# The experts of a routed layer on one core: half-depth chunks, gathers shared by four experts, a second pass for slots 65 to 96

## Chip, core and metric
The kernel runs on one core of a Trainium2 chip, as one launch. The metric is the device time in microseconds. All data are f32. TensorE multiplies, VectorE (DVE in the rows) and ScalarE (ACT) read its results from PSUM, and SyncE (SP) issues nearly all transfers.

## What is computed
Two transformer blocks stand in a row, for 256 tokens of width 1024. The change touches only the mixture of experts in the second:

```
logits = xt @ w_router + b_router             # 256 tokens, 32 experts
top_val, top_idx = lax.top_k(logits, 4)
gates = softmax(top_val)
# for each expert e and its tokens xb:
hdn = xb @ w_up[e] + b_up[e]                  # 1024 x 2048
gate_h = minimum(hdn[:, :1024], 7.0)
up_h = clip(hdn[:, 1024:], -7.0, 7.0)
act = (up_h + 1.0) * gate_h * sigmoid(1.702 * gate_h)
y = act @ w_down[e] + b_down[e]               # 1024 x 1024
out[tok] += y * gate
```

Behind it come a layer norm and a gated product with `w_ple_gate`. The weights of one expert are 12.6 MB, those of all 32 are 403 MB of the 602 MB that the kernel reads.

## The kernel before
The blocks ahead of the experts are left as they are. At their end the router writes MSK (which token goes to which expert), POS (its slot in the expert, by a matmul with a triangle), GTE (its gate) and HTM, the tokens with the token index on the partitions. FLAG holds, for each expert, whether it has at most 64 tokens, and whether any has over 128. In that last case all engines branch to the `dense` code, which runs every expert on all 256 tokens. Else, for each expert, each engine branches to the narrow or to the broad form of `expert`. The narrow code of all experts lies in a row; the broad forms lie behind it, reached by a jump and left by another.

Weights come in chunks of 2 MB, six an expert: four of `w_up` and two of `w_down`. An up chunk c holds, for the full depth of 1024, 256 features (as pairs of gate and up columns), a down chunk 512 outputs. They go to a ring of eight places (parts of BIG, RG and SM1; `R.turn`, L1120). SP issues chunk i when `s_used` has reached i - 7 (L2834), that is when the chunk eight places earlier has been used. TensorE raises `s_used` after each chunk's products.

The narrow form, by TensorE's lines: L1198 puts the biases of two chunks into PSUM (32 rows deep). L1203 multiplies the 64 gathered tokens (stationary, 64 columns) with the chunk: the two halves of its columns go to partitions 0 to 63 and 64 to 127, as pairs of 64-wide tiles. After four chunks, L1157 turns the activations (`activated`), L1132 (`gather`, `picked`) picks the next expert's tokens by a product with SEL, L1214 turns SELG, which has the gates in it, and L1139 (`gather_turn`, `upright`) turns the picked tokens after ScalarE has copied them to XT. L1227 are the down products. L1239 scatters: YV times the turned SELG (SCT) is added to the output sums in banks 0 to 3 (`accap`). L1163 (`biases`) adds the down biases of all experts at once, in expert 24 (`BIASES`).

VectorE makes SEL for the next expert (`select`, L2520), SELG (L2537, L2540), the activation from each chunk (L2560, L2561, L2564, L2566) and the copies of turned blocks (L2569, L2571). ScalarE does the sigmoid (L1846), the copies of the gathered tokens (L1382, L1831) and of the down products to YV (L1852).

The broad form has 128 token slots: the products are 128 wide, unpaired, with 512 columns, and take the same weights twice as long. PSUM banks 4 to 7 serve all of this in turn (`take` waits for a bank to be free, `read_out` for a bank to be read).

Of the kernel before, what the change touches and what calls it, by code (L numbers as in the profile page):

```python
# [12 lines left out]
NEXP = 32  # L13
# [104 lines left out]
def build(nc, A, out):  # L118
    (T1, W1), (T2, W2) = smalls()
    ctx = ExitStack()  # L120
    with ctx:
# [16 lines left out]
        BD = sb("BDN", 1024, 32)  # L138
# [239 lines left out]
        BIASES = 24  # L378
# [8 lines left out]
        GTT = STAT[0:32, 1024:1280]  # L387
# [7 lines left out]
        XG = [XS_[:, 2048 + 1024 * i:3072 + 1024 * i].rearrange("p (k s) -> p k s", k=8) for i in range(2)]  # L395
        AV = CAT_[:, 0:1024]
        AVT = CAT_[:, 1024:2048]
        YV = CAT_[:, 2048:3072]
        XT = CAT_[:, 2560:3072]
        SEL = CAT_[:, 3072:3328].rearrange("p (a s) -> p a s", a=2)  # L400
        SELG = CAT_[:, 3328:3584].rearrange("p (a s) -> p a s", a=2)
# [34 lines left out]
        def _(pe):  # L436
# [673 lines left out]
            for tt in range(2):  # L1110
                m = pe.transpose(banks[b][0:32, tt * 128:tt * 128 + 128], GTE[:, tt, :], ID2)
# [10 lines left out]
            def expert_chunk(ex, c):  # L1122
                i = 6 * ex + c
                s, nth = R.get(("expert", ex, c), R.turn[i % 8])
                pe.wait_ge(s_landed[s], 16 * nth)
                return ring(s).rearrange("p (k n) -> p k n", k=8)

            def picked(b, part):

                for tt in range(2):  # L1130
                    for half in range(2):
                        m = pe.matmul(banks[b][64 * half:64 * half + 64, :], SEL[:, tt, 64 * part:64 * part + 64],  # L1132
                                      HTM[:, tt, 512 * half:512 * half + 512], start=tt == 0, stop=tt == 1)
                return m

            def upright(b):

                for i in range(4):
                    m = pe.transpose(banks[b][:, 128 * i:128 * i + 128], XT[:, 128 * i:128 * i + 128], ID2)  # L1139
# [7 lines left out]
            def gather_turn(ex):  # L1147
                read_out(("xt", ex))
                b = take(("xg", ex))
                upright(b).then_inc(s_full[b], 1)  # L1150

            def activated(ex, half, wd):
                b = take(("at", ex, half))
                pe.wait_ge(s_av, 4 * ex + 2 * half + 2)
                for i in range(wd // 128):
                    c, hh = (2 * half + i // 2, i % 2) if wd == 512 else (2 * half + i, 0)
                    m = pe.transpose(banks[b][:, i * 128:i * 128 + 128], AV[:, c * 256 + hh * 128:c * 256 + hh * 128 + 128], ID2)  # L1157
                m.then_inc(s_full[b], 1)

            def biases():  # L1160

                for d in range(8):
                    pe.matmul(accap(d), BD[0:32, d * 128:d * 128 + 128], GTT, start=False, stop=False, skip_group_check=True)  # L1163

            def half_of(b, h, sides):

                return banks[b][64 * h:64 * h + 64, 0:256] if sides == 2 else banks[b][:, :]

            def expert(ex, broad):
                Xg = XG[ex % 2]  # L1170
                cap = 128 if broad else 64
                sides = 1 if broad else 2
                wd = 512 if broad else 256
# [6 lines left out]
                if ex == BIASES:  # L1180
                    biases()
                read_out(("xg", ex))
                if broad:
                    b = F.pool[F.turn % 4]
                    pe.wait_ge(s_free[b], F.n[b])
                    pe.wait_ge(s_selg, ex + 1)
                    picked(b, 1).then_inc(s_more, 1)
                    pe.wait_ge(s_mcopy, 2 * ex + 1)
                    upright(b).then_inc(s_more, 1)
                    pe.wait_ge(s_mcopy, 2 * ex + 2)  # L1190
                for c in range(4):
                    if c % 2 == 0:
                        for q in c, c + 1:
                            b = take(("up", ex, q), quiet=True)
                            rows = slice(32 * q, 32 * q + 32)
                            onehot = ID2[rows, 32 * q + ex:32 * q + ex + 1].broadcast_to([32, cap])
                            for h in range(sides):
                                pe.matmul(half_of(b, h, sides), onehot, BUPR[rows, h * wd:h * wd + wd], start=True, stop=False)  # L1198
                    w = expert_chunk(ex, c)
                    b, n, m = F.at["up", ex, c]  # L1200
                    for k in range(8):
                        for h in range(sides):
                            i = pe.matmul(half_of(b, h, sides), Xg[:, k, 0:cap], w[:, k, h * wd:h * wd + wd], start=False, stop=k == 7)  # L1203
                            if not broad and c == h == 0 and k < 2:
                                i.then_inc(s_more, 1)
                    i.then_inc(s_used, 1)
                activated(ex, 0, wd)
                if ex + 1 < NEXP:
                    gather(ex + 1)
                activated(ex, 1, wd)  # L1210
# [5 lines left out]
                if ex + 1 < NEXP:  # L1216
                    gather_turn(ex + 1)
                T_ = AVT[:, 0:8 * cap].rearrange("p (k s) -> p k s", k=8)
                for c in range(2):
                    w = expert_chunk(ex, 4 + c)  # L1220
                    b = take(("dn", ex, c), quiet=True)
                    if c == 0:
                        read_out(("at", ex, 0))
                        read_out(("at", ex, 1))
                    for k in range(8):
                        for h in range(sides):
                            m = pe.matmul(half_of(b, h, sides), T_[:, k, :], w[:, k, h * wd:h * wd + wd], start=k == 0, stop=k == 7)  # L1227
                    m.then_inc(s_used, 1)
                read_out(("sc", ex))
                for c in range(2):  # L1230
                    read_out(("dn", ex, c))
                    for j in range(4):
                        if broad:
                            d, rows = 4 * c + j, slice(0, 128)
                            lh = YV[:, d * 128:d * 128 + 128]
                        else:
                            d, rows = 4 * c + 2 * (j % 2) + j // 2, slice(64 * (j % 2), 64 * (j % 2) + 64)
                            lh = YV[rows, c * 256 + (j // 2) * 128:c * 256 + (j // 2) * 128 + 128]
# [1662 lines left out]
def layout(inp):  # L2901
# [7 lines left out]
    A = {}  # L2909
# [67 lines left out]
```

## Time and profile before

| | us |
|---|---|
| median of 3 runs (2348.63 to 2351.63) | 2349.51 |
| span of the profiled execution | 2345.1 |
| TensorE busy (matmul) | 2265.2, 97% |
| VectorE busy | 815.0, 35% |
| ScalarE busy | 499.8, 21% |
| GpSimd busy | 154.2, 7% |
| HBM, mean over the span | 256 GB/s |

The span is from the first to the last instruction of one profiled execution, whose own total is not given beside it; the median lies 4.4 us above the span. The experts take the time from about 1347 us to 2304 us. A busy share of TensorE counts matmuls in flight. In the last third of the span the transfers run at 426 or 427 GB/s, above the 108 to 200 of most of the first half.

### The profile page before, as it was taken

How to read it: one execution, taken by the hardware profiler on the slowest of the kernel's cores; microseconds unless marked ns; L12 is line 12 of the kernel's file. 1: busy time of each engine (PE TensorE's matmuls, PEld its weight loads, DVE VectorE, ACT ScalarE, POOL GpSimd, SP SyncE). 2: the span in 40 equal slices, each digit the busy share in tenths (PEclk: the TensorE clock that was granted, in tenths of full speed). 3: DMA queues.
4: the chain of work that ended last, by engine and by line, in shares of the span. 5: the costliest groups of instructions: out<-in, count | busy, mean ns of one | idle time of the engine just before them, and what ended most of it. 6: DMA issues, size and time to landing. Idle time of an engine off the chain costs nothing.

```text
span 2345.1 us, 34269 instructions
## 1 busy us (share of the span) xinstructions
PE 2265.2 (97%) x14376; PEld 1662.3 (71%) x14376; DVE 815.0 (35%) x2072; ACT 499.8 (21%) x1180; POOL 154.2 (7%) x162
## 2 busy tenths in 40 slices
PE   7999999999999999999999999999999999999998
PEld 4777888888887788887688845666665555565556
DVE  2245554578425420005664321222222222222224
ACT  3255411100024432002443211111111111111113
POOL 1000111144301000000000000000000000000000
PEclk9999999999999999999999999999999999999999
DMA  9733223234325444344332777999999999999993
GB/s 376 276 108 108 108 72 108 72 126 162 108 84 200 182 177 148 144 150 180 131 143 109 295 288 310 426 427 425 427 427 426 427 427 426 427 426 426 427 426 124
DMA packets 44196, 601.60 MB, mean 257 GB/s; under 512 B 4704, under 2 KB 7392, under 8 KB 7808
## 3 DMA queue, kind: packets, MB, share of 16 engines
q1 hardware_dynamic: 43696, 595.40, 62.8%
q10 hardware_dynamic: 336, 3.87, 0.4%
q8 instruction: 120, 1.97, 0.3%
q14 instruction: 44, 0.36, 0.0%
HBM read 598.20 MB, written 1.05 MB: 256 GB/s over the span
## 4 chain that ended last, share of the span: by engine, by line
PE 82%; DMA 13%; DVE 2%; ACT 2%; issue 1%; POOL 0%; SPq 0%; POOLq 0%; PEldq 0%; DVEq 0%; ACTq 0%
PE PS L1203 14%; PE PS L957 8%; PE PS L1227 8%; DMA RG<-in_w_up 7%; PE PS L702 7%; PE PS L737 6%; PE PS L686 5%; PE PS L789 5%; DMA BIG<-in_w_up 4%; PE PS L650 3%; PE PS L535 3%; PE PS L775 2%; PE PS L1239 2%; PE PS L1132 2%; PE PS L474 2%; PE PS L1331 1%
## 5 line engine op out<-in xcount | busy, mean ns | idle before, releaser
L2560 DVE TENSOR_SCALAR STAT<-PS 128x128 f32<-128x128 f32 (+1 forms) x128 | 37.9, 296 | 668.4 <-PE PS L1203 668.4
L1203 PE MATMUL PS<-BIG,XS 128*64 128x256 f32 (+1 forms) x2016 | 236.3, 384 | 6.1 <-DMA BIG<-in_w_up 6.1
L1203 PEld LDWEIGHTS PS<-BIG,XS 128*64 128x64 f32 (+1 forms) x2016 | 145.2, 138 | 95.1 <-issue 17.9
L1203 PE MATMUL PS<-RG,XS 128*64 128x256 f32 (+1 forms) x1520 | 178.0, 384 | 12.2 <-DMA RG<-in_w_up 10.2
L957 PE MATMUL PS<-XS,RG 128*128 128x256 f32 x768 | 172.1, 382 | 5.0 <-DVE XS L1997 4.1
L1382 ACT ACTIVATE BIG<-PS 128x256 f32<-128x256 f32 (+2 forms) x197 | 82.2, 432 | 441.9 <-PE PS L702 138.9
L1203 PEld LDWEIGHTS PS<-RG,XS 128*64 128x64 f32 (+1 forms) x1520 | 107.9, 137 | 80.4 <-DMA RG<-in_w_up 15.8
L957 PEld LDWEIGHTS PS<-XS,RG 128*128 128x128 f32 x768 | 145.5, 191 | 26.9 <-issue 6.9
L1846 ACT ACTIVATE STAT<-STAT 128x128 f32<-128x128 f32 (+1 forms) x128 | 40.1, 313 | 570.2 <-DVE STAT L2560 570.2
L1963 DVE TENSOR_SCALAR HOLD<-PS 128x256 f32<-128x256 f32 x27 | 11.4, 423 | 382.0 <-PE PS L510 277.9
L686 PE MATMUL PS<-HN,RG 128*128 128x256 f32 x576 | 125.1, 379 | 1.0 <-ACT HN L1431 1.0
L1227 PE MATMUL PS<-BIG,CAT 128*64 128x256 f32 (+1 forms) x992 | 120.9, 387 | 0.1
L686 PEld LDWEIGHTS PS<-HN,RG 128*128 128x128 f32 x576 | 109.3, 190 | 16.5 <-issue 1.7
L789 PE MATMUL PS<-BIG,RG 128*128 128x256 f32 x512 | 110.7, 379 | 0.0
L789 PEld LDWEIGHTS PS<-BIG,RG 128*128 128x128 f32 x512 | 97.3, 190 | 13.2
L2700 POOL TENSOR_TENSOR HN<-HN 128x256 f32<-128x256 f32 x84 | 63.2, 753 | 631.7 <-ACT HN L1410 207.7
L1227 PEld LDWEIGHTS PS<-BIG,CAT 128*64 128x64 f32 (+1 forms) x992 | 73.6, 139 | 42.5 <-issue 10.0
L1227 PE MATMUL PS<-RG,CAT 128*64 128x256 f32 x768 | 86.4, 381 | 0.4 <-DVE CAT L2569 0.4
L1382 ACT ACTIVATE CAT<-PS 128x512 f32<-128x512 f32 (+2 forms) x74 | 32.7, 442 | 216.3 <-PE PS L789 103.8
L702 PE MATMUL PS<-HN,RG 128*128 128x256 f32 x336 | 77.3, 379 | 0.0
L1227 PEld LDWEIGHTS PS<-RG,CAT 128*64 128x64 f32 x768 | 54.2, 137 | 28.1 <-issue 3.1
L535 PE MATMUL PS<-HN,RG 128*128 128x256 f32 x320 | 73.1, 382 | 0.0
(374 smaller groups left out, 3427.9 us busy)
## 6 DMA issues: line engine op xcount, KB each, us to landing
BIG<-in_w_up SPq DMA_DIRECT2D x64, 2048.0 KB, 30.5
RG<-in_w_up SPq DMA_DIRECT2D x48, 2048.0 KB, 31.3
BIG<-in_w_down SPq DMA_DIRECT2D x32, 2048.0 KB, 32.0
RG<-in_w_ff SPq DMA_DIRECT2D x31, 2048.0 KB, 8.1
RG<-in_w_ada SPq DMA_DIRECT2D x24, 2048.0 KB, 8.3
RG<-in_w_down SPq DMA_DIRECT2D x24, 2048.0 KB, 34.5
RG<-in_w_in SPq DMA_DIRECT2D x23, 2048.0 KB, 8.2
SM<-in_w_up SPq DMA_DIRECT2D x16, 2048.0 KB, 31.3
```

The source lines that it names most:

```text
L474: m = pe.matmul(banks[b][32 * g:32 * g + 32, :], SILK[:, 32 * k:32 * k + 32], w[:, k, :], start=k < 4, stop=k >= 4)
L535: m = pe.matmul(banks[b][:, 0:256], w[:, k, c0:c0 + 128], N[:, k, :], start=k == 0, stop=k == 7)
L650: m = pe.matmul(banks[b][:, 0:256], w[:, k, 128 * (n % 4):128 * (n % 4) + 128], own(CAT, s)[:, k, :], start=i == 0, stop=i == 7)
L686: m = pe.matmul(banks[b][:, 0:256], w[:, k, 128 * n:128 * n + 128], own(HN, s)[:, k, :], start=k == 0, stop=k == 7)
L702: m = pe.matmul(banks[b][:, 0:256], w[:, k, :], a[:, k, :], start=not first and k == 0, stop=k == 3, skip_group_check=True)
L737: return pe.matmul(banks[b[j]][:, 256 * half:256 * half + 256], w, a, start=first and half == 0, stop=last, skip_group_check=True)
L789: m = pe.matmul(banks[b][:, 0:256], w[:, k, :], own(FFH, s)[:, k, :], start=k == 0, stop=k == 31)
L957: m = pe.matmul(banks[b][:, 0:256], w[:, k, 128 * n:128 * n + 128], src[:, k, 0:256], start=k == 0, stop=k == 7)
L1203: i = pe.matmul(half_of(b, h, sides), Xg[:, k, 0:cap], w[:, k, h * wd:h * wd + wd], start=False, stop=k == 7)
L1227: m = pe.matmul(half_of(b, h, sides), T_[:, k, :], w[:, k, h * wd:h * wd + wd], start=k == 0, stop=k == 7)
L1382: i = act.activation(dst, banks[b][rows, part], fn)
L2700: S.up(pool.tensor_tensor(H[:, i, :], H[:, i, :], H[:, k, :], ALU.add))
```

## The change
In words:

- An up chunk now holds half of the depth (512) for 512 gated features (1024 columns), a down chunk half of the depth for all 1024 outputs. The products keep their pairs of 64-wide tiles, now with 512 columns instead of 256. Two chunks fill one PSUM bank together.
- The gather puts 256 features of the tokens of four experts into XG in one group of four 128-deep matmuls, already the right way up, and is done once an expert (`gather((ex,), ex % 4)`): of the four experts held in XG, one is replaced, a quarter at a time. There is no turning any more. Ahead of the loop three such gathers run, the fourth in the second chunk of expert 0.
- An expert with 65 to 96 tokens does its first 64 as all do, and the others in a second pass with four 32-wide tiles (`more_picked`, `more_upright`, `more_biases`, `more_up`, `more_turned`, `more_down`, `more_scatter`). Over 96 tokens lead to the dense code.
- The scatter of an expert runs in the next expert's head, behind its upper biases. YV is copied in one piece of 512 columns.
- The down biases are added ahead of the loop (`lower_biases`), from 128 partitions.

```diff
-            def gather(ex):
-                pe.wait_ge(s_sel, ex + 1)
-                b = take(("xt", ex))
-                picked(b, 0).then_inc(s_full[b], 1)
+            def gather(key, j):
+
+                b = take(("xg",) + key)
+                for i in range(2):
+                    for tt in range(2):
+                        m = pe.matmul(banks[b][:, 256 * i:256 * i + 256], HTM[:, tt, 256 * j + 128 * i:256 * j + 128 * i + 128],
+                                      SEL[:, tt, :], start=tt == 0, stop=tt == 1)
+                m.then_inc(s_full[b], 1)
+
+            def lower_biases():
+
+                for j in range(2):
+                    for q in range(4):
+                        rows = slice(32 * q, 32 * q + 32)
+                        pe.matmul(accap(2 * q + j), BD[rows, 128 * j:128 * j + 128], GTT[rows, :], start=j == 0, stop=False,
+                                  skip_group_check=True)
+
+            def upper_biases(ex):
+
+                for s in range(2):
+                    b = take(("up", ex, s), quiet=True)
+                    for h in range(2):
+                        q = 2 * s + h
+                        rows = slice(32 * q, 32 * q + 32)
+                        pe.matmul(banks[b][64 * h:64 * h + 64, :], ID2[rows, 32 * q + ex:32 * q + ex + 1].broadcast_to([32, 64]),
+                                  BUPR[rows, :], start=True, stop=False)
...
+            def more_up(b, c, w):
+
+                xg = XG2.rearrange("p (k s) -> p k s", k=8)
+                for kk in range(4):
+                    for q in range(4):
+                        part = w[:, kk, 512 * (q // 2):512 * (q // 2) + 512].rearrange("p (g n) -> p g n", g=2)
+                        m = pe.matmul(banks[b][32 * q:32 * q + 32, 256 * (c // 2):256 * (c // 2) + 256], xg[:, 4 * (c % 2) + kk, :],
+                                      part[:, :, 128 * (q % 2):128 * (q % 2) + 128], start=False, stop=c == 3 and kk == 3,
+                                      skip_group_check=True)
                 return m
...
+                upper_biases(ex)
...
                 if broad:
-                    b = F.pool[F.turn % 4]
...
+                    more_picked(ex, b2)
+                if ex:
+                    scatter(ex - 1)
+                    read_out(("xg", ex - 1))
...
+                if broad:
+                    more_upright(ex, b2)
+                    more_biases(ex, b3)
                 for c in range(4):
...
+                    for kk in range(4):
...
+                        for h in range(2):
+                            i = pe.matmul(banks[b][64 * h:64 * h + 64, :], XG[:, 4 * (c % 2) + kk, 64 * r:64 * r + 64],
+                                          w[:, kk, 512 * h:512 * h + 512], start=False, stop=c % 2 == 1 and kk == 3)
...
+                        i = more_up(b3, c, w)
                     i.then_inc(s_used, 1)
...
+                pe.wait_ge(s_av, 2 * ex + 1)
+                activated(take(("at", ex, 0)), 0)
+                if broad:
+                    pe.wait_ge(s_mcopy, 7 * ex + 3)
                 if ex + 1 < NEXP:
-                    gather(ex + 1)
-                activated(ex, 1, wd)
+                    pe.wait_ge(s_sel, 2 + min(ex, NEXP - 5))
+                    gather((ex,), ex % 4)
...
+                if broad:
+                    more_turned(ex, b2)
+                    pe.wait_ge(s_mcopy, 7 * ex + 6)
...
-                dve.tensor_copy(XT, banks[b][:, :]).then_inc(s_mcopy, 1)
...
+            for j in range(3):
+                gather(("first", j), j)
...
-            gather_turn(0)
+            lower_biases()
...
-            dve.tensor_scalar(FLAG[0:1, 32:33], SV[0:1, 410:411], 128.0, None, ALU.is_gt).then_inc(s_flag, 1)
+            dve.tensor_scalar(FLAG[0:1, 32:33], SV[0:1, 410:411], 96.0, None, ALU.is_gt).then_inc(s_flag, 1)
```

VectorE forms the activation twice an expert on 256 columns instead of four times on 128, and in an expert with over 64 tokens a third time for the second pass. Its `select` makes one operation of 2 x 64 columns with the slot number compared to POS, which holds zero for a token that isn't routed to the expert. The number of bytes is the same in all transfers.

## Rows read from the trace of the kernel before

**Rows 1.** Busy time by stretch of the experts: engines, clock, DMA share, GB/s.
```profile
core 0: us, PE busy (x) PEld busy (x) DVE busy (x) ACT busy (x) POOL busy (x), PEclk, DMA share, GB/s
1343.00:1443.00 100.00, 93.93 (x490) 49.48 (x490) 22.75 (x76) 13.00 (x27) 0.00 (x0) 0.99 0.67 256
1443.00:1812.00 369.00, 366.74 (x3200) 222.93 (x3196) 85.40 (x306) 42.29 (x106) 0.00 (x0) 1.00 1.01 426
1812.00:2288.00 476.00, 452.04 (x3888) 272.32 (x3888) 102.45 (x367) 51.28 (x128) 0.00 (x0) 1.00 1.01 427
```

**Rows 2.** The chain that ended last: start us, us, what (experts 4, 14 and 30).
```profile
1493.37 7.06 PE PS L1203 x64
...
1779.16 33.05 DMA RG<-in_w_up
...
2252.64 35.69 DMA RG<-in_w_up
```

**Rows 3.** Timeline, SP's issues: start us, us, line, what.
```profile
1424.09 7.19 SPq L2795 DMA_DIRECT2D BIG<-in_w_up  x2
1441.27 3.78 SPq L2795 DMA_DIRECT2D RG<-in_w_up  x2
...
1459.57 13.36 SPq L2795 DMA_DIRECT2D BIG<-in_w_up  x4
```

**Rows 4.** Timeline, TensorE in narrow expert 4 and the head of expert 5.
```profile
1508.37 1.94 PE L1132 MATMUL PS<-XS,CAT 128*64 128x512 f32 x8
...
1510.24 0.44 PE L1157 MATMUL PS<-MODT,CAT 128*128 128x128 f32 x2
...
1518.65 2.00 PE L1239 MATMUL PS<-STAT,CAT 64*128 64x256 f32 x16
...
1520.58 0.66 PE L1198 MATMUL PS<-CAT,MODT 32*64 32x256 f32 x8
...
1521.17 3.67 PE L1203 MATMUL PS<-RG,XS 128*64 128x256 f32 x32
```

**Rows 5.** Timeline, from the first selection to the first chunk.
```profile
1346.32 0.54 DVE L2520 TENSOR_SCALAR CAT<-HOLD,MISC 128x64 f32<-128x64 f32 x2
...
1347.11 1.94 PE L1132 MATMUL PS<-XS,CAT 128*64 128x512 f32 x8 [0.87 <-DVE CAT L2520]
...
1351.67 7.13 PE L1203 MATMUL PS<-BIG,XS 128*64 128x256 f32 x64
```

**Rows 6.** Timeline, TensorE where the broad expert 1 begins and ends.
```profile
1377.02 2.00 PE L1239 MATMUL PS<-STAT,CAT 64*128 64x256 f32 x16
1378.95 1.94 PE L1132 MATMUL PS<-XS,CAT 128*64 128x512 f32 x8
...
1430.76 3.62 PE L1239 MATMUL PS<-STAT,CAT 128*128 128x256 f32 x16
...
1434.30 0.66 PE L1198 MATMUL PS<-CAT,MODT 32*64 32x256 f32 x8
...
1438.43 6.26 PE L1203 MATMUL PS<-RG,XS 128*64 128x256 f32 x54 [2.03 <-issue]
```

**Rows 7.** 32-wide tiles (timeline), and full matmuls of 256 columns (chain).
```profile
21.69 1.92 PE L474 MATMUL PS<-RG,SM 128*32 128x512 f32 x16 [0.64 <-DMA RG<-in_w_ada]
...
1250.32 3.46 PE PS L957 x16
```

**Rows 8.** Timeline, VectorE's activation chain and a ScalarE eviction in expert 1.
```profile
1406.35 0.42 DVE L2560 TENSOR_SCALAR STAT<-PS 128x256 f32<-128x256 f32 x1 [6.38 <-PE PS L1203]
...
1407.67 0.42 DVE L2566 TENSOR_TENSOR CAT<-HOLD,STAT 128x256 f32<-128x256 f32 x1
...
1430.96 0.60 ACT L1852 ACTIVATE CAT<-PS 128x512 f32<-128x512 f32 x1 [6.27 <-PE PS L1227]
```

**Rows 9.** Timeline, the last chunk's products in expert 31.
```profile
2298.15 3.67 PE L1227 MATMUL PS<-SM,CAT 128*64 128x256 f32 x32
```

**Rows 10.** Instruction queue in 1812 to 2288 us: packets, MB, share.
```profile
q8 instruction: 32, 0.52, 0.4%
```

More of the change, by code:

```diff
@@ L1160, in biases @@
[L1160 to L1167, printed above, removed]
+                return ring(s).rearrange("p (k n) -> p k n", k=4)
+            def gather(key, j):
[5 more added lines that the diff above has]
+                m.then_inc(s_full[b], 1)
@@ new lines, in activated, with scatter @@
+            def activated(b, s):
+                for i in range(2):
+                    m = pe.transpose(banks[b][:, 128 * i:128 * i + 128], AV[:, 256 * s + 128 * i:256 * s + 128 * i + 128], ID2)
+                m.then_inc(s_full[b], 1)
+            def scatter(ex):
+                read_out(("sc", ex))
+                read_out(("dn", ex))
+                for j in range(4):
+                    for h in range(2):
+                        rows = slice(64 * h, 64 * h + 64)
+                        m = pe.matmul(accap(4 * h + j), YV[rows, 128 * j:128 * j + 128], SCT[rows, :], start=False,
+                                      stop=ex == NEXP - 1, skip_group_check=True)
+                m.then_inc(s_scat, 1)
@@ new lines, in more_turned, with more_down @@
+            def more_turned(ex, b):
+                pe.wait_ge(s_mcopy, 7 * ex + 5)
+                for s in range(2):
+                    pe.transpose(banks[b][:, 128 * s:128 * s + 128], AV2[:, 128 * s:128 * s + 128], ID2)
+                for tt in range(2):
+                    m = pe.transpose(banks[b][:, 256 + 128 * tt:384 + 128 * tt], SELG2[:, tt, :], ID2)
+                m.then_inc(s_more, 1)
+            def more_down(b, c, w):
+                for kk in range(4):
+                    for q in range(4):
+                        m = pe.matmul(banks[b][32 * q:32 * q + 32, 0:256], TS2[:, 128 * c + 32 * kk:128 * c + 32 * kk + 32],
+                                      w[:, kk, 256 * q:256 * q + 256], start=c + kk == 0, stop=c == 1 and kk == 3)
+                return m
@@ L1169, in expert, with more_scatter @@
+            def more_scatter(ex):
+                pe.wait_ge(s_mcopy, 7 * ex + 7)
+                for j in range(2):
+                    for q in range(4):
+                        rows = slice(32 * q, 32 * q + 32)
+                        pe.matmul(accap(2 * q + j), YV2[rows, 128 * j:128 * j + 128], TS2[rows, 256:512], start=False, stop=False,
+                                  skip_group_check=True)
             def expert(ex, broad):
-                Xg = XG[ex % 2]
-                cap = 128 if broad else 64
@@ L1172, in expert @@
[L1172 to L1173 removed]
+                r = ex % 4
                 if ex + 1 < NEXP:
@@ L1224, in expert @@
                         read_out(("at", ex, 1))
-                    for k in range(8):
-                        for h in range(sides):
-                            m = pe.matmul(half_of(b, h, sides), T_[:, k, :], w[:, k, h * wd:h * wd + wd], start=k == 0, stop=k == 7)
-                    m.then_inc(s_used, 1)
[L1229 to L1238, printed above, removed]
-                        m = pe.matmul(accap(d), lh, SCT[rows, :], start=ex == 0 and d % 2 == 0, stop=ex == NEXP - 1,
-                                      skip_group_check=True)
@@ L1241, in expert @@
-                m.then_inc(s_scat, 1)
+                    for kk in range(4):
+                        i = 256 * c + 128 * (kk % 2) + 64 * (kk // 2)
+                        for h in range(2):
+                            m = pe.matmul(banks[b][64 * h:64 * h + 64, :], AVT[:, i:i + 64], w[:, kk, 512 * h:512 * h + 512],
+                                          start=c + kk == 0, stop=c == 1 and kk == 3)
+                    if broad:
+                        read_out(("at", ex, 1))
+                        m = more_down(b4, c, w)
@@ L1863, in dense @@
                     act.activation(SG[:, f % 2, :], GH[:, f % 2, :], ACT.Sigmoid, scale=1.702).then_inc(s_dsg, 1)
-            gathered(0)
+            for j in range(3):
+                gathered(("first", j), j)
             act.wait_ge(s_flag, 1)
@@ L2570, in expert @@
+                for s in range(2):
+                    b = full(("at", ex, s))
+                    dve.tensor_copy(AVT[:, 256 * s:256 * s + 256], banks[b][:, 0:256]).then_inc(s_free[b], 1)
                 b = full(("sc", ex))
                 dve.tensor_copy(SCT, banks[b][:, 0:256]).then_inc(s_free[b], 1)
+                if broad:
+                    dve.wait_ge(s_more, 3 * ex + 3)
+                    dve.tensor_copy(TS2, banks[b2][:, :]).then_inc(s_mcopy, 1)
+                    dve.wait_ge(s_used, 6 * ex + 6)
+                    dve.tensor_copy(YV2, banks[F.at["at", ex, 1][0]][:, 0:256]).then_inc(s_mcopy, 1)
```

278 lines of the change are left out of this document (142 added, 136 removed).

## Prediction

> **What bounds the kernel now.** I read the stretches first. From 1443 us to 2288 us the DMA engines are busy all the time at 426 to 427 GB/s, while TensorE is busy 367 of 369 us before 1812 and only 452 of 476 us after [rows 1]: two limits lie close together, and the second half is the transfers' alone. The chain says the same: the up chunk on which TensorE waits until 1812.2 was issued at 1779.2, the one it waits for until 2288.3 was issued at 2252.6 [rows 2]. Between those two landings lie 16 experts, 96 chunks of 2 MB: 476.1 / 96 = 4.96 us a chunk, 29.76 us an expert. TensorE's own period is 27.8 us (expert 4's first product at 1493.37, expert 5's at 1521.17) [rows 2, 4]. So work saved inside a narrow expert only lengthens its wait for the next chunk.
>
> What can move the end is when the stream becomes gapless. Chunk i is issued when chunk i-8 has been used. Issue time less 4.96 i is largest where the last gap ends: chunk 18 issued at 1424.09 gives 1334.8, chunk 20 at 1441.27 gives 1342.1 [rows 3]; the chunks behind give less (24, issued at 1459.57, 1340.5). Hence the end of the stream hangs on the moment at which the first chunk of expert 2 is used. Between 1343 and 1443 the DMA share is only 0.67 [rows 1]: expert 1, the only one with over 64 slots, runs 128 wide and unpaired, 53.7 us from 1377.02 to 1430.76 [rows 6], against 29.8 us of transfers.
>
> **The change, part by part, as a shift of the issue of chunk 20.** Times are of the profiled execution (span 2345.1 us); the median 2349.51 us lies 4.4 us above the span, and I carry that over.
>
> Start. Selection becomes two 256-wide VectorE operations of 0.42 [rows 8] in place of two of 0.27 [rows 5]: +0.3. Before, 4.56 us pass from the first gather matmul at 1347.11 to the first chunk at 1351.67 [rows 5]. New: three gathers of four 256-column, full-depth matmuls. Sixteen records of that form, 8 matmuls, take 3.46, so 0.432 each [rows 7] and 1.75 a gather with its edge: 5.2. The lower biases (8 matmuls, 32 deep, 128 wide) follow, then the upper biases (4, 512 columns). Four 32-deep matmuls of 256 columns take 0.59 (1520.58 to 1521.17) [rows 4], so four overlap, with 0.16 at the edge: 1.0 for each of the two. Together 7.2, so +2.6. If the lower ones did not overlap, 3.5 instead of 1.0. First use: +2.9.
>
> Expert 0. Added: the fourth first gather 1.75, and the rolling gather 1.75 where the old gather took 1.87 (1508.37 to 1510.24). Gone: the second bias group 0.59 and the turning 0.6. The products stay at four half-width pairs' worth of columns: 7.0 for two chunks (7.06 in [rows 2]); half as many weight loads save at most 0.1 each two. Sum +0.4, so chunk 13's issue +3.3.
>
> Expert 1. From the last down product of expert 0: upper biases 1.0, 32-wide picking 1.0, scatter 1.95 [rows 4], turning 0.45, second biases 1.0: 5.4. Each chunk is 3.5 of 64-wide pairs plus 16 matmuls 32 wide in fours. Are fours concurrent? Eight 32-wide matmuls of 512 columns take 1.92; one after another they would take 8 x 0.86 = 6.9 [rows 7]. So 4 x 0.43 + 0.2 = 1.9, a chunk 5.45 and not 7.0; six are 32.7. Between up and down: turning 0.36, a new wait of TensorE on VectorE (the activation chain of the second half, 1.74 + 0.12 [rows 8], and two more reads of 0.42 of the 65-to-96 bank) some 2.4, gather 1.75, turnings 1.3, a wait of about 0.9 for the TS2 copy (estimate, from 0.60 for a 512-column ScalarE eviction [rows 8]). Behind the down products: YV2 copy 0.6 and the second scatter 1.0. Sum 5.4 + 32.7 + 6.7 + 1.6 = 46.4 against 53.7: -7.3. Queued behind the new waits are the down products and thus the issue of chunks 18 and 19; they give 1330 by the rule above and stay uncritical.
>
> Expert 2's head. Before: unpaired scatter 3.54, biases 0.59, 2.03 of "issue" after the return from the broad code, first chunk: 10.4 to the issue at 1441.2 [rows 3, 6]. New: 1.0 + 1.95 + 2.03 + 3.5 = 8.5: -1.9.
>
> Issue of chunk 20: 3.3 - 7.3 - 1.9 = -5.9. The bounds: all waits of the broad body covered, -9; two more stalls of the 2.03 kind and the slower biases, +1.
>
> Stream. The narrow expert has 134 matmul records where it had 242. The instruction queue moved 0.52 MB in the 16 experts of that stretch [rows 10], TensorE's part perhaps 0.4. Halving it frees 0.2 MB, 0.5 us at 427 GB/s, 0.9 over the stage: -0.9 (0 to -1.2).
>
> Tail. The last chunk's products end 3.67 after 2298.15 [rows 9]; the last up chunk to the first down product takes some 0.3 more (VectorE's chain is 256 wide), covered by the two landings of 4.96 between. Before, the scatter began at once, since half of YV was out. Now it waits for one 512-column eviction, 0.60 + 0.15: +0.8. Only in the last expert is it bare; in the others the next upper biases (1.0) hide it, and where they don't, it costs up to 0.75 of TensorE's slack. That slack grows: new TensorE period 14.0 + 0.36 + 1.75 + 0.77 + 7.0 + 1.0 + 1.95 = 26.8, so 2.9 us under the 29.76. The biases at expert 24 leave, worth nothing there. SP only follows uses; its order, POOL and the ending stay.
>
> Sum: -5.9 - 0.9 + 0.8 = -6.0, so 2339.1 us of span, 2343.5 us.
>
> On tiles: [rows 7] shows fours of one shape overlapping within one group. The Trainium skill, "TensorEngine Tiling (Array Packing)", Key Properties, says that changing the tiling mode drains the engine; the new chunk of expert 1 changes it twice, 12 times in all. The 0.16 to 0.22 us by which groups exceed their columns' time in the trace agree with a small drain, so by the rule too the sum stays.
>
> **The rivals.**
> (a) The gain is eaten at the front: same within 0.2%. The fork into the sparse code had an eviction to hide behind; now biases follow directly, and the broad body is longer. Each stall of the 2.03 kind [rows 6] is a third of the gain. Two, or the bare lower biases, give -6.0 + 2.5 to 4.1: 2346 to 2347.6. For it: such a stall exists. Against: the first operation of the broad code (1378.95) follows the scatter before it (1377.02 and 1.95) without a gap [rows 6]. Chance 0.30. The Trainium skill, "Runtime: NRT & Kernel Launch", Instruction fetch mechanics, says that a taken branch out of the fetched window costs a stall; the 2.03 agrees.
> (b) Slower: the 32-wide fours lose their overlap when mixed with 64-wide pairs in expert 1. There are 24 fours in its chunks. Serial, each costs 1.3 more, +31, so 2374. It decides from 0.44 us more a four (10.7 us in all, for +0.2%). Against: [rows 7]. Chance 0.08.
> (c) The change doesn't do what it says: over 96 slots in an expert the dense code runs. Dense costs 192 full matmuls of 0.432, 83 us, an expert, so some +1700. The routing worked out from the reference gives at most 76 slots (expert 1), and the trace shows one broad expert. Chance 0.01.
> (d) More: broad waits covered and no stall on return, -9 to -11: 2338.5 to 2340.5. Chance 0.08.
> The forecast, 2340.5 to 2345, has 0.53.
>
> **The numbers.** 0.2% is 4.7 us, about what a measurement can tell: the line is 2344.8. Nearly all of the forecast and (d) lie below it: faster 0.60; (a) and the forecast's rim: same 0.30; (b), (c) and an unforeseen +11: slower 0.10. Range 2338.5 to 2350.5: it takes (d) and (a) and leaves (b) and (c) out.
>
> **What would show it.** Chunk 20 issued near 1435.4 with the first chunk used near 1358.2; expert 1 from last down product to YV2's scatter 46 us, its chunks 5.45; TensorE's first wait for a chunk by expert 12 instead of 15; 4.95 us a chunk between landings; last scatter 0.8 later behind its products. It is wrong if a later chunk than 20 becomes the critical one, if the chunks of expert 1 exceed 5.9, or if the pace of the stream changes by more than 0.02 us a chunk (3.4 us over the 172 left).

## The result and the profile after

| us | before | changed |
|---|---|---|
| median (lowest to highest) of 4 runs each | 2349.07 (2346.01 to 2351.63) | 2331.05 (2329.14 to 2332.87) |
| span of the profiled execution | 2345.1 | 2329.2 |
| TensorE busy, matmuls | 2265.2, 97% | 2224.1, 95% |
| instructions | 34269 | 27569 |

The ratio is 0.9925, 95% interval 0.9911 to 0.9939: by it the changed kernel is 17.6 us faster (14 to 21; the two medians lie 18.0 apart), where 6.0 was forecast. The direction held, the size was too small by a factor of two to three, and the time lies below the range.

The span fell by 15.9 us. I cut it at four moments that both traces have: the first gather matmul; the issue of chunk 20; the moment at which TensorE gets the last up chunk (chunk 189); the end. The rows of the changed kernel (timeline; start us, us, then as before):

```profile
1344.83 5.42 PE L1138 MATMUL PS<-CAT,XS 128*128 128x256 f32 x24 [0.73 <-DVE CAT L2693]
1350.18 1.15 PE L1147 MATMUL PS<-STAT,BDN 32*128 32x256 f32 x16
1351.26 1.09 PE L1157 MATMUL PS<-CAT,MODT 32*64 32x512 f32 x8
1352.27 3.65 PE L1275 MATMUL PS<-BIG,XS 128*64 128x512 f32 x16
...
1430.60 3.76 SPq L2888 DMA_DIRECT2D RG<-in_w_up  x2
...
2271.60 3.65 PE L1275 MATMUL PS<-RG,XS 128*64 128x512 f32 x16 [1.24 <-DMA RG<-in_w_up]
```

and that of the kernel before for the third moment (the others are in [rows 5, 3]):

```profile
2288.38 1.95 PE L1203 MATMUL PS<-RG,XS 128*64 128x256 f32 x16 [1.23 <-DMA RG<-in_w_up]
```

| stretch | before | changed | difference | forecast |
|---|---|---|---|---|
| start to first gather | 1347.11 | 1344.83 | -2.3 | 0 |
| first gather to issue of chunk 20 | 94.16 | 85.77 | -8.4 | -6.2 |
| issue of chunk 20 to last up chunk | 847.1 | 841.0 | -6.1 | -0.9 |
| last up chunk to end | 56.7 | 57.6 | +0.9 | +0.8 |

(The -6.2 is the forecast's -5.9 less the +0.3 that lies ahead of the first gather.) The first line is code that the change leaves alone. The router's 32 matmuls took 6.74 us in one trace, at a granted clock of 0.70, and 5.12 in the other, at 0.95; that is 1.6 of the 2.3 us:

```profile
1335.26 6.74 PE L1089 MATMUL PS<-SM,HN 128*128 128x32 f32 x32 [0.96 <-ACT HN L1813]
```
```profile
1334.38 5.12 PE L1093 MATMUL PS<-SM,HN 128*128 128x32 f32 x32 [0.96 <-ACT HN L1892]
```

In the twelve later profiles the first gather lay between 1343.1 and 1347.9, for kernels of either kind. So the change itself is -8.4 - 6.1 + 0.9 = -13.6 us. Two terms are to be explained: 2.2 us too many in the front, 5.2 in the stream.

Expert 1, the broad one, in the changed kernel (TensorE's timeline):

```profile
1377.88 1.09 PE L1157 MATMUL PS<-CAT,MODT 32*64 32x512 f32 x8
1378.90 1.07 PE L1183 MATMUL PS<-XS,CAT 128*32 128x256 f32 x16
1379.90 2.00 PE L1171 MATMUL PS<-STAT,CAT 64*128 64x256 f32 x16
...
1383.20 3.65 PE L1275 MATMUL PS<-RG,XS 128*64 128x512 f32 x16
1386.78 1.93 PE L1211 MATMUL PS<-RG,SM 128*32 128x256 f32 x32
...
1407.71 1.99 PE L1138 MATMUL PS<-CAT,XS 128*128 128x256 f32 x8 [2.28 <-DVE HOLD L2644]
...
1411.37 3.65 PE L1312 MATMUL PS<-BIG,CAT 128*64 128x512 f32 x16 [0.79 <-DVE CAT L2658]
...
1422.88 1.15 PE L1239 MATMUL PS<-CAT,SM 32*128 32x256 f32 x16 [0.55 <-DVE SM L2660]
1423.96 1.09 PE L1157 MATMUL PS<-CAT,MODT 32*64 32x512 f32 x8
1424.97 2.00 PE L1171 MATMUL PS<-STAT,CAT 64*128 64x256 f32 x16
1426.90 4.51 PE L1275 MATMUL PS<-RG,XS 128*64 128x512 f32 x20
```

From 1377.88 to 1423.96 are 46.1 us (forecast 46.4, before 53.7). Eight fours of 32-wide tiles are 32 matmuls in 1.93 us, in the midst of 64-wide pairs: they run side by side. The waits for VectorE are 2.28, 0.79 and 0.55. And in the last line expert 2 begins without the 2.03 us of "issue" that stood there before [rows 6].

In the second half the stream rules even more (TensorE busy 524 of 572 us, the last three columns are clock, DMA share and GB/s; then three steps of the chain that ended last):

```profile
1700.00:2272.00 572.00, 524.21 (x2586) 195.51 (x2584) 97.62 (x266) 38.95 (x77) 0.00 (x0) 1.00 1.01 427
```
```profile
1645.88 35.20 DMA RG<-in_w_up
...
1704.57 35.26 DMA BIG<-in_w_up
...
2236.30 35.26 DMA RG<-in_w_up
```

TensorE first waits for a chunk in expert 10 (forecast: by expert 12), before in expert 15, at 1812.2:

```profile
1646.87 3.65 PE L1275 MATMUL PS<-RG,XS 128*64 128x512 f32 x16 [1.03 <-DMA RG<-in_w_up]
```

From the wait for chunk 69, until 1681.13, to that for chunk 189, until 2271.60, lie 120 chunks: 4.92 us each, before 4.96. A DMA share of 1.01 at 426 to 427 GB/s stands in both kernels' rows, so neither of these columns shows the difference. The queue that fetches instructions does (1443 to 2260 us, packets and MB; before, then changed):

```profile
q1 hardware_dynamic: 23837, 347.32, 100.1%
q8 instruction: 55, 0.90, 0.4%
q14 instruction: 12, 0.10, 0.0%
```
```profile
q1 hardware_dynamic: 23925, 348.56, 100.4%
q8 instruction: 31, 0.51, 0.3%
q14 instruction: 9, 0.07, 0.0%
```

q8 brings pages of 16 KB; their number follows TensorE's instructions, so I take them for TensorE's. 24 pages fewer, and 1.24 MB more of data in the same 817 us. By bytes, 24 pages are 0.39 MB, 0.9 us at 427 GB/s. The stream gained 6.1.

### The profile page after: what moved, and what is told of

Its sections match the earlier page's. It is cut to its first block, busy times and chain, and to the rows that moved or that the text cites. A ratio compares the mean times of both kernels' runs of the same rounds, so it can differ in the third digit from the quotient of the medians.

```text
span 2329.2 us, 27569 instructions
## 1 busy us (share of the span) xinstructions
PE 2224.1 (95%) x11292; PEld 1450.0 (62%) x11292; DVE 771.6 (33%) x1789; ACT 463.3 (20%) x1056; POOL 154.1 (7%) x162
## 4 chain that ended last, share of the span: by engine, by line
PE 78%; DMA 18%; DVE 2%; ACT 1%; issue 0%; POOL 0%; SPq 0%; POOLq 0%; PEldq 0%; DVEq 0%; ACTq 0%
PE PS L1275 11%; DMA RG<-in_w_up 9%; PE PS L961 8%; DMA BIG<-in_w_up 8%; PE PS L706 7%; PE PS L1312 6%; PE PS L741 6%; PE PS L690 5%; PE PS L793 5%; PE PS L654 3%; PE PS L539 3%; PE PS L779 2%; PE PS L1138 2%; PE PS L1171 2%; PE PS L478 1%; PE PS L1412 1%
## 5 line engine op out<-in xcount | busy, mean ns | idle before, releaser
L2632 DVE TENSOR_SCALAR STAT<-PS 128x256 f32<-128x256 f32 x64 | 27.2, 424 | 709.1 <-PE PS L1275 688.6
L1275 PE MATMUL PS<-BIG,XS 128*64 128x512 f32 x1024 | 230.2, 599 | 23.6 <-DMA BIG<-in_w_up 23.6
L1275 PE MATMUL PS<-RG,XS 128*64 128x512 f32 x768 | 172.6, 597 | 20.2 <-DMA RG<-in_w_up 20.2
L1275 PEld LDWEIGHTS PS<-BIG,XS 128*64 128x64 f32 x1024 | 70.4, 137 | 173.1 <-issue 125.9
L961 PEld LDWEIGHTS PS<-XS,RG 128*128 128x128 f32 x768 | 146.6, 193 | 26.8 <-issue 6.9
L1921 ACT ACTIVATE STAT<-STAT 128x256 f32<-128x256 f32 x64 | 26.6, 416 | 592.8 <-DVE STAT L2632 592.8
L1275 PEld LDWEIGHTS PS<-RG,XS 128*64 128x64 f32 x768 | 52.1, 136 | 131.7 <-issue 92.2
L690 PEld LDWEIGHTS PS<-HN,RG 128*128 128x128 f32 x576 | 109.3, 190 | 16.5 <-issue 1.7
L1312 PE MATMUL PS<-BIG,CAT 128*64 128x512 f32 x512 | 115.1, 598 | 0.8 <-DVE CAT L2658 0.8
L1312 PE MATMUL PS<-RG,CAT 128*64 128x512 f32 x384 | 86.5, 597 | 0.0
L1312 PEld LDWEIGHTS PS<-BIG,CAT 128*64 128x64 f32 x512 | 34.3, 136 | 69.8 <-issue 60.0
L654 PE MATMUL PS<-CAT,RG 128*128 128x256 f32 x320 | 71.5, 381 | 0.0
L706 PEld LDWEIGHTS PS<-HN,RG 128*128 128x128 f32 x336 | 63.8, 190 | 8.7
```

The costliest lines, as they stand in the source:

```text
L654: m = pe.matmul(banks[b][:, 0:256], w[:, k, 128 * (n % 4):128 * (n % 4) + 128], own(CAT, s)[:, k, :], start=i == 0, stop=i == 7)
L690: m = pe.matmul(banks[b][:, 0:256], w[:, k, 128 * n:128 * n + 128], own(HN, s)[:, k, :], start=k == 0, stop=k == 7)
L706: m = pe.matmul(banks[b][:, 0:256], w[:, k, :], a[:, k, :], start=not first and k == 0, stop=k == 3, skip_group_check=True)
L961: m = pe.matmul(banks[b][:, 0:256], w[:, k, 128 * n:128 * n + 128], src[:, k, 0:256], start=k == 0, stop=k == 7)
L1275: i = pe.matmul(banks[b][64 * h:64 * h + 64, :], XG[:, 4 * (c % 2) + kk, 64 * r:64 * r + 64], w[:, kk, 512 * h:512 * h + 512], start=False ...
L1312: m = pe.matmul(banks[b][64 * h:64 * h + 64, :], AVT[:, i:i + 64], w[:, kk, 512 * h:512 * h + 512], start=c + kk == 0, stop=c == 1 and kk ...
```

## The experiments

The disputed points: is the stream's gain due to the number of instructions, and why more than their bytes; is the front's extra gain due to the stall after the return; what are the scatter's place and the broad expert worth. The theory I began with: each page costs the stream about 0.25 us, since 6.1 / 24 = 0.25. Its rivals: the gain is the luck of one profile; it comes from the scatter or from lower load on TensorE; it is another effect of the larger instructions.

### The changed kernel again

> The changed kernel as it is, as a control for the runs beside it. Expected: 0.9925 of before, so -16 to -19 us; landings of up chunks two experts apart 58.7 us, with one in four or five of these periods 1.5 us longer (4.92 us a chunk); no stall of TensorE where it returns from the broad code; chunk 20 issued at about 1430.6. If the 2.3 us by which the router's end lay earlier in the first profile were luck of the clock, the first gather matmul lies anywhere between 1344.5 and 1347.5 here.

2334.28 us (2329.56 to 2335.39), ratio 0.9933 (0.9911 to 0.9954). Issue of chunk 20 to last up chunk: 840.9 us with 31 pages. The term is no luck of one profile. First gather to chunk 20 took 87.47, with the gather behind the 2.28 us wait at 3.54 instead of 1.99 us, at a granted clock of 0.55.

### Products in halves: more instructions, the same work

```diff
-    i = pe.matmul(banks[b][64 * h:64 * h + 64, :], XG[...], w[:, kk, 512 * h:512 * h + 512], ...)
+    for n0, n1 in ((0, 256), (256, 512)) if ex >= 3 and not (c % 2 == 1 and kk == 3) else ((0, 512),):
+        i = pe.matmul(banks[b][64 * h:64 * h + 64, n0:n1], XG[...], w[:, kk, 512 * h + n0:512 * h + n1], ...)
```

(and so for the down products)

> The changed kernel, but from expert 3 on 40 of the 48 products of an expert are made as two of 256 columns (the last group of each accumulation stays whole). That brings 80 more matmul records and 80 more weight loads an expert, 0.74 of what the change had taken away, and costs TensorE under 0.3 us of the 2.9 us that it has to spare. Theory 1 (the stream goes at the pace of its most loaded DMA engine, and instruction fetches load it): the instruction queue between 1443 and 2260 us moves from 31 to some 50 pages, two-expert periods with 1.5 us more become nearly twice as frequent, 4.95 us a chunk, and the time is 4.4 us (3 to 6) above the control. Theory 2 (the pace changed for the sake of the new chunks or of the order of their use): the pace stays 4.92 and the time within 0.7 us of the control.

```profile
q8 instruction: 48, 0.79, 0.4%
```

48 pages, and the stream took 845.1 us, 4.2 more than with 31: 0.25 us a page again, close to the 4.4 expected. TensorE's work is the same, and the front did not move (86.38). The medians alone (2335.51, ratio 0.9946, 0.9926 to 0.9967) don't tell it from the kernel run beside it (2334.28), so the forecast of the time, 4.4 above that one, was missed there: in the two profiled executions the start, the front and the tail took 3.7 us of the 4.2 back. At an equal mean granted clock it shows: the four executions of this form at 0.996 or 0.997 have a median of 2334.98, the four of the changed kernel at 0.996 one of 2331.05, 3.9 less. The verdict rests on these and on the cut traces.

### The scatter in its own expert

```diff
                 if ex:
-                    scatter(ex - 1)
                     read_out(("xg", ex - 1))
...
                     more_scatter(ex)
+                scatter(ex)
```

> The changed kernel, but each expert scatters at its own end, ahead of the next biases. TensorE then waits some 0.75 us an expert for the copy of YV. My sum (a narrow expert has 2.9 us to spare against the transfers): no change against the control within 0.7 us, apart from chunk 20, which is issued up to 1.5 us later (two bare copies, of experts 0 and 1): +1 us. Rival (TensorE's periods still count): 31 x 0.75 = +23 us.

2333.76 us (2331.15 to 2338.97), ratio 0.9936 (0.9915 to 0.9957), stream 840.9. TensorE now waits 0.79 us for ScalarE ahead of each scatter, and in the narrow experts this costs nothing: it comes out of the wait for the next chunk. The front is less clear. In this profile the issue of chunk 20 lies 91.38 us behind the first gather, 3.9 later than in the control; 2.6 of it are the three first gathers, at a granted clock of 0.67, and 1.3 lie behind them, where up to 1.5 was expected. The medians (2333.76 and 2334.28) don't show it. So the place of the scatter is worth at most the 1 us that was expected.

### The kernel before without a broad expert

```diff
-            dve.tensor_scalar(FLAG[0:1, 0:32], banks[b][0:1, 64:96], 64.0, None, ALU.is_le)...
+            dve.tensor_scalar(FLAG[0:1, 0:32], banks[b][0:1, 64:96], 256.0, None, ALU.is_le)...
```

> The kernel before, but the narrow form is taken for every expert, so expert 1 leaves out its slots above 64: its output isn't complete. Theory 1 (the end hangs on the moment from which the transfers have no gap): the 53.7 us of expert 1 become 27.9, chunk 8 is then the one that decides (issued 1355.4, less 4.96 x 8 = 1315.7 against 1342.1), so -26 us, -1.1%. Rival (TensorE's own sum also limits the stage, since it falls behind): -16 us or less. No stall of 2.03 us in expert 2.

2320.10 us (2317.19 to 2325.78), ratio 0.9873 (0.9847 to 0.9900): 31 us less, 26 were expected. Some of that is clock: the one execution at 0.996 took 2317.19, 26.6 less than the 2343.75 of the kernel before at that clock. With the expert narrow, the last gap ends at chunk 8, issued at 1361.35 (in this profile late, since the first gather and products ran at a granted clock of 0.56), and the stall of 2.03 us is gone. So to within a microsecond the front's 26 us were the price of expert 1's width.

### The kernels with the broad expert late

The experts are renamed in the layout and the router alike, so that the broad one comes as the 18th (expert 17); the same is computed.

```diff
+    turned = np.roll(np.arange(32), 16)
+    for n in ("w_up_2", "w_down_2", "b_up_2", "b_down_2"):
+        f[n] = f[n][:, turned]
+    for n in ("w_router_2", "b_router_2"):
+        f[n] = f[n][..., turned]
```

> The changed kernel with the experts relabelled by 16 in the packing of the weights (the router's columns too), so that the one with 76 tokens comes as number 17 instead of 1. Nothing else changes: the same work and bytes. Theory 1 (only the moment from which the transfers have no gap counts; late in the stream a ring of eight chunks, some 35 us from issue to landing, covers an expert that takes 43 us): chunk 8 decides, issued near 1356 us, less 4.92 x 8 = 1316.6 against 1332.2 with chunk 20, so -15.6 us against the changed kernel, near 2317. Rival (an expert with a second pass costs its 13 us more than 29.5 wherever it stands): within 2 us of the changed kernel.

2317.99 us (2316.92 to 2319.14), ratio 0.9867 (0.9851 to 0.9883), near the 2317 expected. The second pass costs nothing at the end when the ring is full in front of it; in its stretch the stream stays up (425 GB/s):

```profile
1829.00:1875.00 46.00, 42.38 (x350) 18.25 (x352) 8.12 (x22) 2.44 (x5) 0.00 (x0) 0.96 1.01 425
1875.00:1890.00 15.00, 10.67 (x80) 4.96 (x74) 1.23 (x4) 0.60 (x1) 0.00 (x0) 0.89 0.98 412
```

It was covered narrowly. Behind the return from the second pass this changed kernel has a stall too, of 3.78 us in the midst of expert 18's scatter (with one of 0.54 where the second pass began), and just behind it the rate falls to 412 GB/s:

```profile
1878.85 0.70 PE L1171 MATMUL PS<-STAT,CAT 64*128 64x256 f32 x3
1883.33 3.09 PE L1171 MATMUL PS<-STAT,CAT 64*128 64x256 f32 x13 [3.78 <-issue]
```

This is the best version found: 13 us below the changed kernel (15.6 were expected), 29 below the kernel before. It hangs on the routing, which only these data fix.

> The kernel before with the same relabelling: its broad expert comes as number 17. Theory 1: chunk 8 decides (1315.7 against 1342.1), -26 us, near 2324; TensorE falls 24 us behind at expert 17 and makes it up at 1.9 us an expert, just by the end, so up to 3 us may be left. The rest of the difference to the relabelled changed kernel is then the pace (6) and no longer the broad expert. Rival as for the changed kernel: no change against before.

2336.99 us (2334.79 to 2346.81), ratio 0.9962 (0.9947 to 0.9977), where 2324 was expected: a miss. The broad code of before is not hidden there:

```profile
1824.84 2.00 PE L1239 MATMUL PS<-STAT,CAT 64*128 64x256 f32 x16
1833.19 3.68 PE L1132 MATMUL PS<-XS,CAT 128*64 128x512 f32 x8 [6.36 <-issue]
...
1880.00:1890.00 10.00, 10.00 (x25) 4.50 (x24) 0.00 (x0) 0.60 (x1) 0.00 (x0) 1.00 0.56 202
```

The jump cost 6.36 us, and the first gather behind it ran at a granted clock of 0.50 (3.68 us, 1.94 at full clock [rows 6]). From its predecessor's scatter to its own (1824.84 to 1890.26) the expert took 65.4 us, and its unpaired scatter takes 1.6 more than a narrow one: 67.0. The stream brings six chunks in 29.8, so TensorE fell 37.2 us behind, more than the some 35 us from issue to landing in a full ring. The stream thinned, to 351 to 387 GB/s from 1850 and to 202 from 1880.

What ends this run is then TensorE and no longer the stream. From 1894 on it waits for no chunk at all; it goes at its own 27.9 to 28.5 us an expert (33.5 in the one that adds the biases), with no idle moment over 0.5 us before the last expert. The expectation had it 24 us behind and level again by the end; from 37.2 it had not caught up: it took the last up chunk, which landed at 2268.84, at about 2277.4. So the rule of the last gap has a condition: TensorE must be level with the stream again before the end.

### The changed kernel without a second pass

> The changed kernel, but with the narrow form for every expert, so expert 1 leaves out its slots above 64: its output isn't complete. It shows what the second pass still costs. Gapless-start theory: chunk 8 decides, 15.6 us off the changed kernel, as the relabelled one had (2318); 2 us less than that if the second pass at expert 17 was fully covered there, since both then run from the same start.

2318.46 us (2317.87 to 2321.78), ratio 0.9884 (0.9864 to 0.9905). With the renamed form at 2317.99, this says that the second pass is wholly covered there. Cut from the issue of chunk 8 to the last up chunk, the two agree as well (901.7 us renamed, 902.25 narrow). The two narrow forms also give a second price for pages: from the issue of chunk 8 to the last up chunk 905.6 us before (61 pages from 1360 to 2260) and 902.25 changed (34 pages), 3.4 us for 27 pages, 0.12 each; in both, no two first completions of the chunks behind chunk 8 lie over 6 us apart, so the streams had no gap. So 0.25 us is no constant.

### What in a page costs: GpSimd's instructions

GpSimd idles in the experts. From expert 3 on, it was given 160 tiny operations an expert; then one operation of the same width; then 40 tiny ones.

```diff
+            for ex in range(3, NEXP):
+                pool.wait_ge(s_used, 6 * ex)
...
+                for i in range(160):
+                    m = pool.memset(SCR[:, i:i + 1], 0.0)
+                m.then_inc(s_nop, 1)
```

> The changed kernel, with 160 memsets of one column an expert on GpSimd, which is idle there, from expert 3 on: as many more instructions as the run with split products had on TensorE. If any engine's instruction fetch loads the DMA engine that sets the pace: +4.2 us between the issue of chunk 20 and the landing of the last up chunk (840.9 without). If only TensorE's fetches go by that one, or if the split products cost in another way than by their fetches: no change within 0.7 us, though an instruction queue moves as many more bytes.

```profile
q8 instruction: 30, 0.49, 0.2%
q14 instruction: 45, 0.37, 0.1%
```

2352.88 us (2350.32 to 2358.31), ratio 1.0025 (1.0011 to 1.0038). The stream took 860.5 us: +19.6 for 36 packets of 8 KB, where 4.2 was expected. Something in these instructions slows the stream; the size was missed again, upwards.

> As the run with 160 memsets of one column an expert on GpSimd, which took 19.6 us more (860.5 instead of 840.9) from the issue of chunk 20 to the landing of the last up chunk; here one memset of 160 columns an expert writes the same bytes. If it was the fetch of the instructions that cost: 841 again, within 1 us. If it was GpSimd's writes: as before, some 860.

2330.85 us, stream 841.0, 10 packets in q14. So it is the number of GpSimd's instructions, not its waits or the bytes that it writes. That they act by being fetched is read from q14's packets and from the completions below.

> The same with 40 memsets of one column an expert. Fetch theory, by bytes: a quarter of 19.6, so 845.8 (844.5 to 847), and the instruction queue that went from 9 to 45 packets between 1443 and 2260 us goes to some 18. If any activity of GpSimd in an expert costs a fixed amount: 860.

2330.65 us. 19 packets in q14, ten more than without, and the stream took 841.5: +0.6, where 4.8 was expected of a fixed price a packet. The price is not linear.

The completions show where the time goes. A chunk's transfer ends in sixteen completions, which I take as one for each of sixteen parts, and TensorE waits for the last. In the trace's completion records, the first of the sixteen keeps 4.895 to 4.897 us a chunk in every kernel of this table. The distance from a chunk's first completion to its last is 1.6 to 2.7 us at chunk 30 and grows, as far as chunk 189, to:

| kernel | pages of q8, packets of q14 | issue of chunk 20 to first completion of chunk 189 | distance to its last | stream |
|---|---|---|---|---|
| changed | 31, 9 | 834.4 | 6.6 | 841.0 |
| GpSimd, 40 | 31, 19 | 834.3 | 7.2 | 841.5 |
| halves | 48, 9 | 834.5 | 10.6 | 845.1 |
| before | 55, 12 | 834.2 | 12.8 | 847.1 |
| GpSimd, 160 | 30, 45 | 834.5 | 26.0 | 860.5 |

The first parts arrive at the same time in all five, within 0.3 us, and the distance is the whole difference between the streams. So not all sixteen parts are late, some fall behind, and each chunk waits for the slowest part. The mean DMA share cannot show that. How many fall behind differs too. At chunk 189 seven parts of the kernel before complete within 2.1 us, one at 8.1 and eight at 10.7 to 12.8: what goes with TensorE's pages falls on about half of the parts. With 160 memsets, fifteen complete by 6.4 us (6.6 in the changed kernel) and a single one at 26.0: what goes with GpSimd's instructions falls on one. That is why ten packets more in q14 cost little: until that part is the slowest, nothing is lost.

The packet records give half of the price. A page of q8 takes 1.07 us (median), where a packet of the weights with the same 16 KB takes 0.61; a packet of q14 takes 0.31 to 0.33. If 24 pages are spread evenly over eight parts, each has 3.2 us more, of the 6.1; 36 packets of q14 on one part are 11, of the 19.4 by which the distance grew (both are estimates from these durations). What the rest is, and whether it is the same part each time, was not measured.

### The stall at the branches: the code's position

96 instructions `pe.sem_inc(s_nop, 1)` on TensorE ahead of the experts move all its later code by 96 instructions.

> The kernel before, with 96 semaphore increments at the start of TensorE's program, while it waits for its first data. They move all of its later code by 96 instructions. If the stall of 2.03 us behind the return from the broad code is a matter of where the code lies in the pages that are fetched, it changes its place or length, or goes. If it belongs to what the code does there, it stays at 10 records into the first chunk of expert 2.

```profile
1428.51 3.62 PE L1241 MATMUL PS<-STAT,CAT 128*128 128x256 f32 x16
1432.05 0.66 PE L1200 MATMUL PS<-CAT,MODT 32*64 32x256 f32 x8
1432.64 7.13 PE L1205 MATMUL PS<-RG,XS 128*64 128x256 f32 x64
```

2341.76 us, one execution. The 2.03 us after the return are gone, and first gather to chunk 20 is 91.50 instead of 94.16.

> The changed kernel with 96 semaphore increments at the start of TensorE's program. In before, the stall behind the return from the broad code (2.03 us) was gone with them. If it depends on where the code lies, the changed kernel may get one here that it hasn't got now: a stall of TensorE of up to 2.1 us with no releaser between 1376 and 1430 us, and a chunk 20 later by it (85.8 to 87.5 us behind the first gather without). If the change itself removed it: none.

```profile
1430.56 0.64 PE L1277 MATMUL PS<-RG,XS 128*64 128x512 f32 x1
1434.04 11.75 PE L1277 MATMUL PS<-RG,XS 128*64 128x512 f32 x46 [2.84 <-issue]
```

2339.76 us, one execution, chunk 20 issued 91.47 us behind the first gather instead of 85.77: the changed kernel gets a stall of 2.84 us in the same place, and slower products behind it (granted clock 0.72 from 1434 to 1440). So its absence there belongs to where the code happens to lie, not to what the change does. The relabelled changed kernel, without added instructions, had 3.78 us behind its return. The shift moved smaller idle moments as well: the kernel before has ten of 0.3 to 0.5 us of "issue" at the heads of narrow experts (3.8 us in all), the shifted one 21 (8.8 us), the changed kernel none. The Trainium skill, "Runtime: NRT & Kernel Launch", Instruction fetch mechanics, says that a taken branch whose target is not within the fetched pages waits for a fetch; the 2.03 and 2.84 us, and their coming and going with the position, agree. For the 6.36 us of the relabelled kernel before no position was tested; it stood in a full stream (422 GB/s from 1827 to 1833), and how much of it goes with that is open. The same section calls the crossing of a page mostly hidden. For TensorE these runs show no more idle time than the moments just named, against 55 pages; for a saturated stream it does not hold, which loses 4.2 us to 17 pages more.

### The medians

The cut gives -13.6, the first comparison -17.6. Each timed execution has its mean granted clock. The 39 executions of the kernel before that ran beside the experiments go from 2342.4 us at 0.996 to 2356.5 at 0.989; its 14 at 0.996 have a median of 2343.75. The four of the changed kernel at 0.996 (2329.56 to 2331.82) have 2331.05: -12.7, next to the cut. None of the ten of the changed kernel was below 0.995, 23 of the 39 were. So the rest of the difference between medians goes with lower clock in the kernel before. Why it meets that more often was not tested.

## Why the prediction was right in its direction and wrong in its size

- What bounds the kernel: right. The end follows the issue of chunk 20. A narrow expert 1, in either kernel, or a late one behind the second pass, moves the end as that rule says. The narrow period is 26.48 us, forecast 26.8, and what that saves goes into the waits for chunks. The one run against the rule is the relabelled kernel before, where TensorE fell too far behind to be level again.
- Start: right. First use of a chunk at 1355.97; with the 2.3 us of the earlier start 1358.3, forecast 1358.2. Expert 0: +0.3 against +0.4 (25.61 us from its first product to the next expert's head, before 25.35 to its scatter).
- Expert 1: right, 46.1 against 46.4, its chunks 5.45. Rival (b), serial fours, fell with the 1.93 us rows. The Trainium skill, "TensorEngine Tiling (Array Packing)", Key Properties, has a change of tiling mode drain the engine; here a change of mode leaves no idle time in the rows of expert 1.
- Expert 2's head: the step that kept the 2.03 us of issue after the return failed. It took a stall that comes and goes with the position of the code for one that belongs to the branch. It is 2.0 of the 2.2 us that the front gained beyond the forecast, and that the changed kernel has no such stall is luck: its shifted form and its relabelled form each have one. Rival (a) counted on two more such stalls.
- Stream: this is the term that was mis-sized, -0.9 against -6.1. The step that failed divided the bytes of the instruction pages by the rate of all sixteen parts of the transfers together. Shown in its place: the chunk waits for its slowest part, and the pages load only some; the distance to the last completion is 12.8 us before and 6.6 changed, which is the 6.1. More instructions alone, with the same work, give back 4.2 us, and 160 more an expert on GpSimd alone cost 19.6. The forecast named a pace that changes by over 0.02 us a chunk as what would make it wrong; it changed by 6.1 / 169 = 0.036.
- Tail: right, +0.9 against +0.8; the scatter behind the last products waits 0.79 us for ScalarE:

```profile
2285.82 2.00 PE L1171 MATMUL PS<-STAT,CAT 64*128 64x256 f32 x16 [0.79 <-ACT CAT L1929]
```

- Rival (d) had the missing stall, but not the stream. The range was built from the bounds of steps that could be read in TensorE's rows, and the stream's bound (0 to -1.2) had only bytes behind it, no row of a fetch's effect.

## What to carry to other kernels

When transfers bind, find the last gap in the stream: the largest issue time less pace times index names the chunk, and only work ahead of it counts; a long item belongs where the ring is full in front of it, as long as it is shorter than what the ring covers and TensorE can be level again by the end. In a saturated stream do not price instruction pages by their bytes at the full rate: look at the distance between a chunk's first and last completion, and prefer few large instructions even on engines that idle. A stall at a branch can belong to the code's position: move the code by some instructions before it is put into a sum.

## What of the hardware was not expected

- A 16 KB page of TensorE's instructions cost the stream 0.12 to 0.25 us, while the same bytes at 427 GB/s are 0.04 us; 36 packets of 8 KB for GpSimd cost 19.6 us, ten 0.6.
- At a DMA share of 1.01 and 427 GB/s in both, the streams still differed by 0.7% in 840 us; the distance between a chunk's first and last completion (6.6 and 12.8 us at chunk 189) showed it, the rate did not.
- The instructions of GpSimd delayed one of sixteen parts (26.0 us, the next 6.4), those of TensorE about half of them. A 16 KB page of q8 took 1.07 us, a 16 KB packet of weights 0.61.
- Behind a jump or a return TensorE lost nothing, 2.03, 2.84, 3.78 or 6.36 us. For the 2.03 and the 2.84 the position of the code was shown to decide. What followed the 6.36 ran at a granted clock of 0.50 (3.68 us instead of 1.94), what followed the 2.84 at 0.72.
